# Two transformer blocks on one core: weight splits, the turning of the attention's probabilities and an output projection in another order

## The reference

```python
# first block
h = rms_norm(x, g[0]); proj = h @ w_in
y_a = hyena_mixer(...); y_b = neighbourhood_attention(...); y_c = short_conv_mixer(...)
merged = gates[0] * (y_a @ w_branch[0]) + gates[1] * (y_b @ w_branch[1]) + gates[2] * (y_c @ w_branch[2])
x = x + rms_norm(merged @ w_out, g[1])                       # norm "r1", then "n2"
mem_n = rms_norm(mem, mem_norm)
x = x + rms_norm(memory_cross_attention(rms_norm(x, g[2]), mem_n, xa_wq, xa_wkv, xa_wo), g[3])   # "r3"
h = rms_norm(x, g[4])                                        # "n4"
u = dwconv3(h @ w_up, w_conv); gate, val = split(u)
x = x + rms_norm((gelu(gate) * val) @ w_down, g[5])          # "r5"
# second block, 16 meta tokens in front
hn = rms_norm(h, attn_norm_2); proj = hn @ w_in_2
h = h + concat(mla_mixer, diff_mixer, swa_mixer) @ w_out_2   # last part of it: "o2"
hn = rms_norm(h, ffn_norm_2)                                 # "n8"
h = h + (silu(hn @ w_gate_2) * (hn @ w_up_2)) @ w_down_2
return rms_norm(h, final_norm)
```

## Time and profile before

| | |
|---|---|
| median of 3 runs | 1954.23 us |
| profiled execution | 1953.56 us |
| its span, first to last instruction | 1951.8 us |
| TensorE busy | 1829.9 us, 94% |
| VectorE busy | 1011.5 us, 52% |
| ScalarE busy | 733.3 us, 38% |
| GpSimd busy | 289.3 us, 15% |
| mean granted clock of TensorE | 0.965 |

### The profile page before, as it was taken

One profiled execution on the slowest core, in us unless ns is written; L12 is line 12 of the kernel. 1 busy time (PEld: TensorE's weight loads), 2 busy tenths in 40 slices (PEclk: granted clock), 3 DMA queues, 4 the chain that ended last, 5 costly groups with the idle time before them and its releaser, 6 DMA issues. The chain is left out here.

```text
span 1951.8 us, 22257 instructions
## 1 busy us (share of the span) xinstructions
PE 1829.9 (94%) x8987; PEld 1464.6 (75%) x8987; DVE 1011.5 (52%) x1517; ACT 733.3 (38%) x1219; POOL 289.3 (15%) x233
## 2 busy tenths in 40 slices
PE   7899999999999978989999999889878989999998
PEld 5678877788888766868888788877655768888887
DVE  6777844444444455358777522674454534444322
ACT  4433344333334433334444322444445533322221
POOL 1023500111102130141111100500100011111000
PEclk9999999999999989989999999898877989999999
DMA  5222322132224320222222222321200122222221
GB/s 185 87 86 87 106 79 76 65 121 95 97 98 164 117 75 33 76 76 87 86 97 97 87 98 87 119 81 68 88 22 32 44 75 88 97 97 97 87 97 54
DMA packets 49829, 171.13 MB, mean 88 GB/s; under 512 B 5882, under 2 KB 8570, under 8 KB 49600
## 3 DMA queue, kind: packets, MB, share of 16 engines
q1 hardware_dynamic: 45216, 155.69, 23.1%
q0 software_dynamic: 3936, 13.51, 2.0%
q10 hardware_dynamic: 576, 0.52, 0.1%
HBM read 165.51 MB, written 4.19 MB: 87 GB/s over the span
## 5 line engine op out<-in xcount | busy, mean ns | idle before, releaser
L308 DVE TENSOR_TENSOR ws_l<-raw,ws_h 128x1024 fp32r<-128x1024 f32 x289 | 387.9, 1346 | 574.3 <-ACT ws_h L300 573.9
L371 PE MATMUL ps<-h_h,ws_h 128*128 128x512 f32 (+1 forms) x1448 | 584.8, 404 | 38.9 <-DVE ws_l L308 13.3
L372 PE MATMUL ps<-h_l,ws_h 128*128 128x512 f32 (+1 forms) x1448 | 572.9, 396 | 0.0
L373 PE MATMUL ps<-h_h,ws_l 128*128 128x512 f32 (+1 forms) x1448 | 571.7, 395 | 0.0
L300 ACT ACTIVATE ws_h<-raw 128x1024 fp32r<-128x1024 f32 x289 | 303.6, 1054 | 490.4 <-PE ps L373 486.8
L371 PEld LDWEIGHTS ps<-h_h,ws_h 128*128 128x128 f32 x1448 | 278.4, 192 | 115.2 <-issue 29.1
L373 PEld LDWEIGHTS ps<-h_h,ws_l 128*128 128x128 f32 x1448 | 278.7, 192 | 62.1
L372 PEld LDWEIGHTS ps<-h_l,ws_h 128*128 128x128 f32 x1448 | 279.2, 193 | 58.4 <-issue 0.2
L371 PE MATMUL ps<-G_h,ws_h 128*128 128x512 f32 (+1 forms) x374 | 143.5, 384 | 4.2 <-DVE ws_l L308 4.2
L372 PE MATMUL ps<-G_l,ws_h 128*128 128x512 f32 (+1 forms) x374 | 143.3, 383 | 0.0
L373 PE MATMUL ps<-G_h,ws_l 128*128 128x512 f32 (+1 forms) x374 | 143.3, 383 | 0.0
(11 more groups left out here) (438 smaller groups left out, 2429.9 us busy)
## 6 DMA issues: line engine op xcount, KB each, us to landing
raw<-in_ffn_up SPq DMA_DIRECT2D x88, 512.0 KB, 3.2
raw<-in_w_merge SPq DMA_DIRECT2D x36, 512.0 KB, 3.2
raw<-in_ffn_down SPq DMA_DIRECT2D x22, 512.0 KB, 3.2
raw<-in_w_down SPq DMA_DIRECT2D x22, 512.0 KB, 3.2
raw<-in_w_hy SPq DMA_DIRECT2D x12, 512.0 KB, 4.8
raw<-in_w_sc SPq DMA_DIRECT2D x12, 512.0 KB, 3.3
raw<-in_fwd SPq DMA_DIRECT2D x8, 512.0 KB, 3.2
raw<-in_w_naqk SPq DMA_DIRECT2D x8, 512.0 KB, 3.2
```

The costliest lines, as they stand in the source:

```text
L308: dve.e.tensor_tensor(w.lo, raw[n % NRAW][:], w.hi, ALU.subtract).then_inc(*lo_made.says(("lo", n)))
L371: pe.e.matmul(o, a.hi, b.hi, start=start, stop=False, skip_group_check=True)
L372: pe.e.matmul(o, a.hi, b.lo, start=False, stop=False, skip_group_check=True)
L373: return pe.e.matmul(o, a.lo, b.hi, start=False, stop=stop, skip_group_check=True)
```

## The change

Five places are edited.

1. *Residual "r1" and queries.* `beside(m)` now stands behind step m in VectorE's program (on ScalarE it stays in front), and is called for m = 1, 2, 3 and 5, which takes in one chunk more, that of the first query tile. The query tiles 0 to 4 take their banks from a ring of their own, of banks whose tiles have been read.
2. *Memory attention.* The diagonal matrices go. VectorE makes a reciprocal per quarter of the tokens and multiplies the quarter's exponentials by it in place, quarter j-1 behind the maximum of quarter j; TensorE transposes the quarters, both halves of the memories one after the other.
3. *Norm's factor.* It is spread between tiles (2,1) and (3,0) instead of between (2,0) and (2,1), in both up-projections.
4. *First way down.* The call for its first chunk moves from behind the last pair to in front of it.
5. *Second output projection.* The blocks go (0..2; 5, 6), (0..2; 7), and then tile by tile for 3 to 7. The calls for its chunks are spread among the additions, behind tiles 1 and 4; the call for the first chunk of the up-projection goes behind all halves of h, the last square behind it.

```diff
-LAST_PARTS = [(m, k) for m in range(7) for k in (5, 6)] + [(m, 7) for m in range(7)] + [(7, k) for k in (5, 6, 7)]
+LAST_PARTS = [(m, k) for m in range(3) for k in (5, 6)] + [(m, 7) for m in range(3)] + [
+    (m, k) for m in range(3, 8) for k in (5, 6, 7)]
...
         for m in range(8):
-            beside(m)
             i, old = rings["dve T"].take(("rs", v, m))
...
             if m > 1:
                 h_rest(nv, m - 2, ngain, dst(m - 2))
+            beside(m)
...
-    Y01_FREE = {"r1": ("mn", 7), "r3": ("xa diag used", 3), "r5": ("off done", "r3")}
+    Y01_FREE = {"r1": ("mn", 7), "r3": ("off done", "r1"), "r5": ("off done", "r3")}
...
+    XA_BESIDE = (1, 2, 3, 5)
...
+        xq_banks = Ring(place, [bank_at["k", 7], bank_at["v2", 0, 0], bank_at["v2", 0, 1], bank_at["r1", 6], bank_at["r1", 7]])
...
-            o = bank(("xq", t), main) if k == 0 else out_of(("xq", t))
+            o = bank(("xq", t), xq_banks) if k == 0 else out_of(("xq", t))
...
-            for kc in range(2):
-                b = bank(("xt", hd, kc), ring)
-                pe.wait_ge(("xa diag", hd))
-                for j in range(4):
-                    i = mm32(b[:, 128 * j:128 * j + 128], xaP[z][:, j, kc * 128:(kc + 1) * 128],
-                             xaD[z][:, 128 * j:128 * j + 128])
-                i.then_inc(*products.says(("done", ("xt", hd, kc)), ("xa diag used", hd)))
-                yield
+            b = [bank(("xt", hd, kc), ring) for kc in range(2)]
+            for j in range(4):
+                pe.wait_ge(("xa over", hd, j))
+                for kc in range(2):
+                    i = pe.e.transpose(b[kc][:, 128 * j:128 * j + 128], xaP[z][:, j, kc * 128:(kc + 1) * 128], ident[:])
+                if j == 3:
+                    i.then_inc(*products.says(("done", ("xt", hd)), ("xa turned", hd)))
+            yield
+            yield
...
         for m in range(5):
-            f.next(8)
+            if m:
+                f.next(8)
...
+            def scaled(j):
+
+                dve.wait_ge(("xP", hd, j))
+                dve.e.reciprocal(s[:, 12 + j:13 + j], s[:, 8 + j:9 + j]).then_inc(*dve_part.says(("xover", hd, j)))
+                dve.wait_ge(("xover", hd, j))
+                dve.e.tensor_scalar(xaP[z][:, j, :], xaP[z][:, j, :], s[:, 12 + j:13 + j], None, ALU.mult).then_inc(
+                    *dve_part.says(("xa over", hd, j)))
...
+                if j:
+                    scaled(j - 1)
                 yield
             yield
-            dve.wait_ge(("xP", hd, 3))
-            dve.e.reciprocal(s[:, 12:16], s[:, 8:12]).then_inc(*dve_part.says(("xover", hd)))
-            dve.wait_ge(("xover", hd), ("xa diag used", hd - 2) if hd > 1 else ("off done", "r1"))
-            for j in range(4):
-                dve.e.tensor_scalar(xaD[z][:, 128 * j:128 * j + 128], ident[:], s[:, 12 + j:13 + j], None,
-                                    ALU.mult).then_inc(*dve_part.says(("xa diag", hd)))
+            scaled(3)
...
-                elif (i, j) == (2, 0):
+                elif (i, j) == (2, 1):
                     spread_tokens(v, bank(("spread", v), rings["seven"]))
...
+        down = Follow(chunk_act)
         for n in range(23):
             f.next(8 if n == 0 else 16 if n < 22 else 0)
+            if n == 22:
+                down.next(8)
...
         for m in range(8):
-            f.next(22)
+            down.next(22 if m else 14)
             outputs_act("r5", m, "n4")
...
+        f.next(8)
+        for m in range(7):
+            squared_x(m)
+            if m < 5:
+                begun(m)
+            if m in (1, 4):
+                f.next(8)
+        for m in range(5, 8):
+            begun(m)
+        rings["f"].next(8)
+        load_roots()
+        squared_x(7)
...
     def out2_dve():
         f = Follow(chunk_dve)
-        f.next(24)
+        f.next(8)
         for m in range(8):
             onto_x("o2", m, ("x", "o2", m), ("x", "pd", m))
-            if m > 1:
+            if 1 < m < 7:
                 h_rest("n8", m - 2, "ffn_norm_2", hm(m - 2))
+            if m in (1, 4):
+                f.next(8)
+        for m in range(5, 8):
+            h_rest("n8", m, "ffn_norm_2", hm(m))
         rings["f"] = Follow(chunk_dve)
         rings["f"].next(8)
-        h_rest("n8", 6, "ffn_norm_2", hm(6))
-        h_rest("n8", 7, "ffn_norm_2", hm(7))
```

More of the change, by code:

```diff
@@ L1486, in xa_pe @@
         for m in (3, 4):
-            tile(bank(("xq", m), main), blocks, 8, hk, ("xq", m), lambda k: ("h", "n2", k))
+            tile(bank(("xq", m), xq_banks), blocks, 8, hk, ("xq", m), lambda k: ("h", "n2", k))
             if m == 3:
@@ L1566, in xa_act @@
                 half_values(0)
[L1567 removed]
+        residual_act("r1", "n2", "ng2", hm, chunk_act, lambda m: chunk_act() if m in XA_BESIDE else None)
         half_values(1)
@@ L1592, in attend @@
                 yield
-                act.wait_ge(("xneg", hd, j), ("xa diag used", hd - 2) if hd > 1 else None)
+                act.wait_ge(("xneg", hd, j), ("xa turned", hd - 2) if hd > 1 else None)
                 act.e.activation(xaP[z][:, j, :], out_of(("xS", hd, j))[:, 0:256], ACT.Exp, bias=s[:, 4 + j:5 + j],
@@ L1792, in finish @@
                 *dve_part.says(("G1", i), ("gone", ("u", i, 0))))
+        down = Follow(chunk_dve)
         for n in range(23):
             f.next(8 if n == 0 else 16 if n < 22 else 0)
+            if n == 22:
+                down.next(8)
             if n == 2:
@@ L1811, in ffn1_dve @@
         rings["dve T"] = Ring(place, (0, 1, 2), ("G1", 21))
-        f = Follow(chunk_dve)
         for m in range(8):
-            f.next(22)
+            down.next(22 if m else 14)
     def ffn1_pool():
@@ L1838, in out2_act, with squared_x, begun @@
         f = Follow(chunk_act)
-        f.next(24)
         rings["f"] = Follow(chunk_act)
-        for m in range(8):
-            if m == 7:
-                load_roots()
+        def squared_x(m):
             act.wait_ge(("x", "o2", m), *(("mix", i) for i in range(8)))
             square("n8", m, x[:, m, :], L, ("D", 1), True, rings["act T"])
+        def begun(m):
             h_part("n8", m, "ffn_norm_2", hm(m), ("x", "o2", m), mix_read(m))
-            if m == 4:
-                rings["f"].next(8)
+        f.next(8)
[10 more added lines that the diff above has]
+        squared_x(7)
     def mix_read(m):
```

9 lines of the change are left out of this document (3 added, 6 removed).

## The result

The changed kernel took 1933.42 us (median of 4 runs, 1931.25 to 1937.78) beside 1954.15 for the kernel before (4 runs): a ratio of 0.9897, 95% interval 0.9876 to 0.9918. The forecast was 1929.5, range 1921 to 1939. The profiled execution took 1932.11 us (span 1930.0, TensorE's mean granted clock 0.967 for 0.965 before), 21.8 us of span less; the forecast for it was 24.1. In 51 later runs the kernel before took 1944.4 to 1958.2 us, 23 of them under 1949, so the four here lie in the upper part of its range.

The account below looks back on a forecast made before the run. TensorE was taken as the bound, at work 1829.9 of 1951.8 us. Terms of -11.2, -2.5, -4.8, +2.1, -4.7 and -3.0 sum to -24.1, taking 1953.56 to 1929.5 us; range 1921 to 1939.

Parts of the forecast that it names:

- Part 1: First residual into the queries: new banks and later splits let TensorE start sooner, -11.2 us.
- less the waits in them start at 691.5 and end at 700.4: Second norm's sum of squares: GpSimd's six additions, freed of their waits, would be done at 700.4 us.
- Part 2: Memory attention: transposes and VectorE multiplications replace the passes by diagonal matrices, -2.5 us (-6 to +1).
- The low stretch added for heads 2 and 3: Memory attention, heads 2 and 3: few short TensorE passes bring one time at the lower clock, costing 1.7 us.
- rival A: VectorE and GpSimd meet more often, delaying path splits; heads 2 and 3 get a second low-clock time; 1937 us, chance 0.22.
- Part 3: Norm factor spread a tile later: second up-projection -4.8 us, first +2.1 because VectorE's chunk split comes late.
- Part 4: First way down: an earlier chunk split removes a 3.03 us gap and 1.7 us of low clock, -4.7 us.
- Part 5: Second output projection: additions tile by tile, TensorE resumes earlier after a gap of 2.5 us, -3.0 us (-5 to 0).
- gaps over 3 us were always followed by one: Odds for TensorE's clock: every gap over 3 us brings a time at the lower clock, priced 1.7 us.
- B: First up-projection's late chunk comes in time and the clock holds after gaps near 2.5 us; 1919.5 us, chance 0.14.
- C: First residual: the bank is free but the three splits keep their old times through ScalarE's order; 1942 us, chance 0.08.
- D: First up-projection: late start never heals, VectorE's two-tile round exceeds TensorE's 11.15 us; 1965 at 2 a round, chance 0.04.

Follow-up runs that it names:

- n2_total_inside: Changed kernel with the second norm's sum of squares taken inside query tile 3, after five of its eight blocks; 1930.6 us, ratio 0.9883 to the kernel before.
- two_splits_held: Changed kernel with VectorE holding the splits of query chunks 4 and 5 until GpSimd's last addition for the second norm; 1934.2 us, ratio 0.9935.
- diagonals_back: Changed kernel with memory attention turned and scaled by diagonal matrices again, in place of multiplications and transposes; 1938.5 us, ratio 0.9934 to the kernel before.
- old_banks: Changed kernel with the banks of query tiles 0 to 4 from the main ring again, the new split order kept; 1926.6 us, ratio 0.9870.
- ends_back: Changed kernel with the first way down's chunk call and the second output projection's order put back as before; 1943.6 us, ratio 0.9970.
- splits_between: Changed kernel with each pair's two chunk splits apart in the first up-projection, one ahead of the pair, one between its tiles; 1952.0 us, ratio 1.0005.
- the repeat: The changed kernel run once more, unedited, beside the kernel before; 1934.7 us, ratio 0.9922.
- both_in: Changed kernel with the second norm's sum inside query tile 3 and first up-projection splits apart, ScalarE's second half before the gelu; 1924.9 us, ratio 0.9863.
- all_in: both_in with one more edit: the second up-projection's third chunk split ahead of the last two halves of h; 1919.3 us, ratio 0.9859.
- old_splits: Changed kernel with the three query chunks split at their old places, the new banks kept; 1946.6 us, ratio 0.9969 to the kernel before.
- n8_spread_early: Changed kernel with the second up-projection's norm factor spread after tile 3 again, the first one's still late; 1940.4 us, ratio 0.9955.

## Why the prediction was right, and where not

The time lay in the range because four of the six terms held within 0.8 us, and the errors of the other two (4.8 and 1.4) together are less than the 9.5 us from the forecast to the end of the range. Chance gave back 2.6 us; the time would have been in the range without it.

- **Part 1, -11.2: wrong by 4.8.** Chunk 1 came at 682.3 (forecast 681.5, or 682.2 with the start 0.7 later), chunk 2 without a wait, and TensorE was at the sum at 700.3 (forecast 699.5, or 700.2). The step that failed is "less the waits in them start at 691.5 and end at 700.4": the additions were freed of their waits, but the step didn't ask what VectorE would do beside them. Its splits of chunks 3 to 5 waited for TensorE's progress and so came behind the additions, from 710.02 on; with TensorE sooner they come from 698.03 on, into the additions, at the price of overlap that the same paragraph had measured. GpSimd ended at 703.1 for 700.4: 0.7 is the later start, 1.5 the last two additions (2.07 and 2.06 us for 1.3), the rest the first two, which met halves of h as before (1.75 and 1.57). The forecast had a wait of 0.9 us in its sum; it was 2.9. No fall of the clock was priced behind it either, and 6.8 us at the low level came: together the wait and the clock took 6.4, by n2_total_inside. The bounds given, 8 to 13.5, left the result out. The lock that the Trainium skill states (SBUF - State Buffer, "Who interferes with whom") agrees with two_splits_held: the last addition took 1.26 us without a split beside it and 2.06 with one. The +0.5 for the bank was 0: the first score product waited 0.60.
- **Part 2, -2.5: right, -3.3** here, and diagonals_back gives 3.1 to 4.6. Head by head -2.7, -0.8 and -0.2 for -2.7, -0.9 and -0.6. The 4 us named for head 0 "if it does not fall" came too: in n2_total_inside and old_banks the clock stayed up there, and the value product starts 3.9 us earlier. The low stretch added for heads 2 and 3 came, 3.4 us long, but cost 0.4 and not 1.7 in this execution. In nine of the twelve with transposes it was 6.8 us, and the whole stretch 1.2 to 1.8 us longer than here: that is the second low stretch of rival A. The multiplication took 0.35 us, between its bounds.
- **Part 3:** first norm +1.9 for +2.1, with the gap where it was placed (4.30 us for 4.4). Second norm, the other term that missed, -3.4 for -4.8: -4.5 by chunk 6, then 1.1 given back by the pace of the products, which the forecast took as unchanged.
- **Part 4, -4.7: exact** in this pair, 3.1 where the clock stays up. **Part 5, -3.3 for -3.0**, with the gap of 2.2 (forecast 2.5).
- **The clock:** "gaps over 3 us were always followed by one" holds in that trace but is no rule (3.04 us in ends_back, no fall). "About every second time" holds for gaps near 2.2: before chunk 2 of the second up-projection, with an unchanged gap of 2.19 to 2.23 us, it fell in 5 of 11 executions, and that stretch took 43.5 to 43.6 us or 42.1: one such fall costs 1.5 us, near the 1.7 taken. Other waits that nearly all executions share: 1.87 us near 110, a fall in 8 of 14; 2.16 near 231, in 5 of 14; 2.57 at query chunk 1, in 8 of 11; 3.4 to 3.9 near 72, in all 14. The wait of 1.87 us was followed by a fall more often than that of 2.16, so the length alone doesn't set the odds.
- **Rivals:** A's first half happened, but at GpSimd's sum and not at the splits on the path; its second, at heads 2 and 3, in most executions but not in this one. B needed chunk 8 in time, and it was 4.30 us late; C didn't occur. D's is real (splits_between), yet the changed kernel kept VectorE's order.
- **Luck:** the -2.6 us between n6 and the output projection were not forecast; the stretch is unedited and varies by 14 us with the clock. Without them the profiled execution would be near 1934.7, which is also the repeat's median. In part 2 it had the shorter of the two low stretches at heads 2 and 3, worth 1.4 us against the middle of the twelve. The four runs of the kernel before, none under 1951.9, helped the ratio too: the repeat's is 0.9922.

## What to carry to other kernels

When a wait is taken off a chain, lay out every engine beside it anew: an operation can now be slowed by neighbours that used to run after it, since the wait had held them back too (the splits of chunks 3 to 5 here). A sum that waits for other engines belongs inside a tile of long products, so that work covers it. Judge an edit of a few microseconds by the stretch that it touches, between two instructions of the bounding engine, and price it with the clock up and down.

## What the runs showed of the hardware

- **A wait followed by one-column passes.** TensorE's wait for the sum of n2 was followed by 6.8 us of low clock in all eight executions that had it (seven waits of 2.90 to 2.92 us, one of 2.12); the like gap of 2.2 us with long products behind it in 5 of 11, and by 3.4 us. With the 16 passes but no wait (n2_total_inside, both_in, all_in, old_banks, old_splits) it stayed up. Whether the passes matter was not tried alone.
- **Two paces at full clock.** In the second up-projection a product comes every 0.2333 us on average in all twelve executions with the late spread, and every 0.2322 in the two with the early one (the kernel before and n8_spread_early); from chunk 6 to the way down that is 212.88 or 211.79 us each time. The output projection's order is not the cause: ends_back kept 212.88. In the first up-projection the late spread gave either pace (189.49 us from chunk 10 on, or 190.40), in programs whose instructions for TensorE are the same up to there (both_in and all_in). So it is not fixed by the program; the cause stays open.
- **Meetings with GpSimd can be arranged.** From 900 to 1060, VectorE's splits take 1459 ns on average in both_in and 1793 in the changed kernel, for the same work: placed apart, they mostly miss GpSimd's product (3 of them take 2.3 us, where 15 do in the changed kernel). The group of both_in, then that of the changed kernel:

```profile
L309 DVE TENSOR_TENSOR ws_l<-raw,ws_h 128x1024 fp32r<-128x1024 f32 x30 | 43.8, 1459 | 21.6 <-ACT ws_h L301 21.6
```
```profile
L309 DVE TENSOR_TENSOR ws_l<-raw,ws_h 128x1024 fp32r<-128x1024 f32 x29 | 52.0, 1793 | 16.0 <-ACT ws_h L301 16.0
```
